# Cross queries and perceptron on unnormalised activations, with the token factor applied later

## The reference

```python
def rms_norm(x, g):
    return x * rsqrt(mean(x * x, axis=-1) + EPS) * g          # EPS = 1e-6

def memory_cross_attention(h, mem_n, wq, wkv, q_g, k_g, wo):
    q = rms_norm((h @ wq).reshape(b, s, XA_HEADS, XA_HEAD_DIM), q_g)
    kv = mem_n @ wkv
    ...

x = x + concatenate([y_a, y_b, y_c]) @ w_out                  # "mix_out"
x = x + memory_cross_attention(rms_norm(x, norm_cross), mem_n, ...)
hm = rms_norm(x, norm_mlp) @ mlp_w1
x = x + square(relu(hm)) @ mlp_w2
```

## Time and profile before

| | |
|---|---|
| median of 3 runs | 1986.47 us (1983.07 to 1989.07) |
| the profiled execution's own time | 1987.62 us |
| its span in the profile | 1985.7 us |
| TensorE busy | 1887.4 us, 95% |
| VectorE busy | 823.4 us, 41% |
| ScalarE busy | 457.4 us, 23% |
| GpSimd busy | 1110.6 us, 56% |
| mean granted TensorE clock | 0.966 of full |

### The profile page before, as it was taken

One profiled execution on the slowest core, in us unless ns is written; L12 is line 12 of the kernel. 1 busy time (PEld: TensorE's weight loads), 2 busy tenths in 40 slices (PEclk: granted clock), 3 DMA queues, 4 the chain that ended last, 5 costly groups with the idle time before them and its releaser, 6 DMA issues.

```text
span 1985.7 us, 27063 instructions
## 1 busy us (share of the span) xinstructions
PE 1887.4 (95%) x9670; PEld 1558.8 (79%) x9670; DVE 823.4 (41%) x1414; ACT 457.4 (23%) x933; POOL 1110.6 (56%) x856
## 2 busy tenths in 40 slices
PE   8999999998999999999998989989889869999998
PEld 4888888887888888888786768877768558887886
DVE  5642615364233333233414865964342653103300
ACT  3121111101222221222201155444122322001200
POOL 3745546496545544445464568752246468767862
PEclk9999999998999999999998989979898979999999
DMA  9423222383223222223222312010122123332331
GB/s 354 129 68 95 69 74 79 91 309 93 78 70 94 83 74 70 67 83 84 79 74 79 95 43 64 22 43 1 43 64 65 42 76 104 96 95 85 102 99 43
DMA packets 279468, 172.76 MB, mean 87 GB/s; under 512 B 5936, under 2 KB 269936, under 8 KB 278384
## 3 DMA queue, kind: packets, MB, share of 16 engines
q1 hardware_dynamic: 272912, 151.01, 26.0%
q10 hardware_dynamic: 6496, 20.93, 3.2%
HBM read 169.69 MB, written 2.10 MB: 87 GB/s over the span
## 4 chain that ended last, share of the span: by engine, by line
PE 88%; DVE 7%; ACT 2%; issue 1%; DMA 1%; POOL 1%; SPq 0%; DVEq 0%; ACTq 0%; POOLq 0%
PE acc L373 16%; PE acc L375 16%; PE acc L374 16%; PE acc L414 3%; PE acc L415 3%; PE acc L416 3%; PE acc L396 3%; PE st L427 3%; PE acc L398 3%; PE acc L397 3%; PE sc L1417 2%; PE ob L1347 2%; PE sc L1397 2%; PE bc L460 2%; DVE conv_out L2263 2%
## 5 line engine op out<-in xcount | busy, mean ns | idle before, releaser
L711 POOL TENSOR_TENSOR wl<-raw,wh 128x512 fp32r<-128x512 f32 x464 | 654.4, 1432 | 19.3
L708 POOL TENSOR_SCALAR wh<-raw 128x1024 fp32r<-128x1024 f32 x232 | 262.9, 1133 | 705.2 <-PE acc L375 312.3
L373 PE MATMUL acc<-hh,wh 128*128 128x512 f32 x816 | 331.7, 407 | 0.0
L375 PE MATMUL acc<-hh,wl 128*128 128x512 f32 x816 | 321.1, 393 | 0.0
L374 PE MATMUL acc<-hl,wh 128*128 128x512 f32 x816 | 320.2, 392 | 0.0
L373 PE MATMUL acc<-Yh,wh 128*128 128x512 f32 x512 | 204.3, 399 | 0.0
L374 PE MATMUL acc<-Yl,wh 128*128 128x512 f32 x512 | 203.2, 397 | 0.0
L375 PE MATMUL acc<-Yh,wl 128*128 128x512 f32 x512 | 203.2, 397 | 0.0
L373 PEld LDWEIGHTS acc<-hh,wh 128*128 128x128 f32 x816 | 155.0, 190 | 33.6 <-issue 1.9
L374 PEld LDWEIGHTS acc<-hl,wh 128*128 128x128 f32 x816 | 155.0, 190 | 33.0 <-issue 2.2
L375 PEld LDWEIGHTS acc<-hh,wl 128*128 128x128 f32 x816 | 154.5, 189 | 33.3
(11 more groups left out here) (411 smaller groups left out, 3061.3 us busy)
## 6 DMA issues: line engine op xcount, KB each, us to landing
raw<-in_att_w_in SPq DMA_DIRECT2D x64, 512.0 KB, 4.0
raw<-in_mlp_w SPq DMA_DIRECT2D x64, 512.0 KB, 3.8
raw<-in_ret_w_in SPq DMA_DIRECT2D x48, 512.0 KB, 3.9
ada_w<-in_ada_w ACTq DMA_DIRECT2D x8, 1536.0 KB, 8.1
raw<-in_w_in SPq DMA_DIRECT2D x23, 512.0 KB, 3.8
ada_w<-in_ada_w SPq DMA_DIRECT2D x16, 512.0 KB, 10.5
raw<-in_ret_w_out SPq DMA_DIRECT2D x16, 512.0 KB, 4.4
raw<-in_att_w_out SPq DMA_DIRECT2D x16, 512.0 KB, 4.1
```

Source lines behind the costliest of these rows:

```text
L373: e.matmul(bank[:, :], wh[:, s, k, :], rhs_high(k), start=(start and k == 0), stop=False)
L375: last = e.matmul(bank[:, :], wl[:, s, k, :], rhs_high(k), start=False, stop=(stop and k == k1 - 1))
L708: e.tensor_scalar(wh[:, s, :, :], raw[:, s, :, :], 1.0, 1.0, ALU.mult, ALU.mult).then_inc(high_done, 1)
L711: low = e.tensor_tensor(wl[:, s, k0:k0 + KT // 2, :], raw[:, s, k0:k0 + KT // 2, :], wh[:, s, k0:k0 + KT // 2, :].bitcast(F32), ALU.subtract)
```

## The change

For "nx": DVE adds a tile of mix_out to xT, ACT at once writes hh = xT times the gain (scale in the copy), DVE forms hl = xT times gain minus hh. No token factor goes in. TensorE's loop over the eight products is written out, and the memory's transposes stand between the products. The pair of queries then waits for the last add and for its tiles. The squares are summed beside that, and their columns go to st behind the pair ("nxcols"). The query roots take EPS (mean(x²) + EPS) in place of EPS, two small operations more. For "nf" the same: hh and hl come straight from xT, squares go to eight tiles of their own (fsq) and are summed by DVE behind the last hl; columns come behind mlp_in0, the root is squared, spread behind the second product of mlp_out0 and copied to fscale, and each output tile of both halves is multiplied by fscale in PSUM before it is added to xT.

```diff
+        def flat_high(e, tag, name, j, g):
+            e.wait_ge(*V.at(f"{name}x{j}"))
+            e.activation(hh[:, j, :], xT[:, j, :], ACT.Copy, scale=sm(g, j, 1)).then_inc(*AC.done(f"{tag}hi{j}"))
+        def flat_add(e, name, j):
+            e.wait_ge(unit_used, U[name] + j + 1)
+            e.tensor_tensor(xT[:, j, :], acc[j % 2][:, :], xT[:, j, :], ALU.add).then_inc(*V.done(f"{name}x{j}"))
+        def flat_low(e, tag, j, g):
+            e.wait_ge(*AC.at(f"{tag}hi{j}"))
+            e.scalar_tensor_tensor(out=hl[:, j, :], in0=xT[:, j, :], scalar=sm(g, j, 1), in1=hh[:, j, :].bitcast(F32),
+                                   op0=ALU.mult, op1=ALU.subtract).then_inc(*V.done(f"{tag}h{j}"))
...
 # ScalarE
-            out_squares(e, "mix_out", 2, 4)
-            for k in range(KT):
+            def memory_out(k):
                 e.wait_ge(*PE.at(f"m{k}"))
                 e.activation(mT[:, k, :], ob[k % 2][:, 0:MEM], ACT.Copy).then_inc(*AC.done(f"m{k}"))
-            norm_highs(e, "nx")
+            for j in range(KT):
+                flat_high(e, "nx", "mix_out", j, "norm_cross")
+                if j >= 2:
+                    e.wait_ge(*V.at(f"mix_outss{j - 2}"))
+                e.activation(sq[:, j % 2, :], xT[:, j, :], ACT.Square).then_inc(*AC.done(f"mix_outsq{j}"))
+                if j:
+                    memory_out(j - 1)
+            memory_out(KT - 1)
+            e.wait_ge(*V.at(f"mix_outss{KT - 1}"))
...
-            out_squares(e, "xa_out", 2, 4)
-            norm_highs(e, "nf")
+            for j in range(KT):
+                flat_high(e, "nf", "xa_out", j, "norm_mlp")
+            for j in range(KT):
+                e.activation(fsq[:, j, :], xT[:, j, :], ACT.Square).then_inc(*AC.done(f"nfsq{j}"))
             for half in range(2):
                 if half:
+                    e.wait_ge(*PE.at("nfbc"))
+                    e.activation(fscale[:, :], bc[:, :], ACT.Copy).then_inc(*AC.done("nfscale"))
...
 # TensorE
+            def out_flat(name, ready, k1, between=None):
                 e.wait_ge(*ready)
+                for j in range(KT):
+                    if j >= 2:
+                        e.wait_ge(*V.at(f"{name}x{j - 2}"))
+                    product(e, acc[j % 2], U[name] + j, U[name] + j, lambda k: Mh[:, k, :], lambda k: Ml[:, k, :], k1=k1)
+                    if between is not None and j:
+                        between(j - 1)
...
-            stream_sums(e, "nx", V.after("mix_outss3", 2))
...
-            norm_spread(e, "nx")
+            out_flat("mix_out", V.at(f"g_lo{GH - 1}"), KT, memory_turned)
+            memory_turned(KT - 1)
+            e.wait_ge(*V.at("mix_outx6"))
+            e.wait_ge(*V.at("mix_outx7"))
...
                 if h == 0:
+                    e.wait_ge(*V.at(f"mix_outss{KT - 1}"))
+                    columns(e, dg, 24, True, True, "nxcols")
                     square_sums(e, "nk", 2)
...
-            stream_sums(e, "nf", V.after("xa_outss3", 2))
-            norm_spread(e, "nf")
+            e.wait_ge(*V.at("xa_outx7"))
...
+                if half == 0:
+                    e.wait_ge(*V.at("nfss"))
+                    columns(e, dg, 0, "first", "last", "nfcols")
                 out_tensor(e, f"mlp_out{half}", [AC.after(f"f{half}r{b + 2}", 4) for b in range(2)],
-                           [V.after(f"f{half}yl3", 2), V.after(f"f{half}yl3", 4)])
+                           [V.after(f"f{half}yl3", 2), V.after(f"f{half}yl3", 4)],
+                           None if half else [lambda: None, lambda: norm_spread(e, "nf")])
...
 # VectorE
-            add_flat("mix_out")
-            norm_roots(e, "nx")
-            norm_vector(e, "nx", lambda k: sm("norm_cross", k, 1))
+            for j in range(KT):
+                flat_add(e, "mix_out", j)
+                flat_low(e, "nx", j, "norm_cross")
+                mix_out_sum(j)
...
-            rsqrt(e, 24, 1.0 / XD, "x_root")
+            e.tensor_scalar(rs[:, 2, 0:NT], st[:, 24:24 + NT], EPS / D, EPS * EPS, ALU.mult, ALU.add).then_inc(*V.done("nxeps"))
+            e.tensor_scalar(rs[:, 1, 16:24], st[:, 16:24], 1.0 / XD, EPS, ALU.mult, ALU.add).then_inc(*V.done())
...
+            roots(e, 0, 24, "x_root")
...
-            add_flat("xa_out")
-            norm_roots(e, "nf")
-            norm_vector(e, "nf", lambda k: sm("norm_mlp", k, 1))
+            for j in range(KT):
+                flat_add(e, "xa_out", j)
+                if j:
+                    flat_low(e, "nf", j - 1, "norm_mlp")
+            flat_low(e, "nf", KT - 1, "norm_mlp")
+            e.wait_ge(*AC.at("nfsq1"))
+            step(e, e.tensor_tensor(dg[:, :], fsq[:, 0, :], fsq[:, 1, :], ALU.add), V)
+            for j in range(2, KT):
+                e.wait_ge(*AC.at(f"nfsq{j}"))
+                step(e, e.tensor_tensor(dg[:, :], dg[:, :], fsq[:, j, :], ALU.add), V, "nfss" if j == KT - 1 else None)
+            def mlp_out(half):
+                c = U[f"mlp_out{half}"]
+                with e.Fori(0, KT // 2) as i:
+                    V.enter(f"mlp_out{half}", i)
+                    for b in range(2):
+                        x = xT[:, bass.ds(i * 2 + b, 1), :]
+                        e.wait_ge(unit_used, c + i * 4 + b + 3)
+                        step(e, e.tensor_tensor(acc[b][:, :], acc[b][:, :], fscale[:, :], ALU.mult), V)
+                        e.tensor_tensor(x, acc[b][:, :].unsqueeze(1), x, ALU.add).then_inc(*V.done(f"mlp_out{half}x{b}"))
+                    V.leave(KT // 2)
```

More of the change, by code:

```diff
@@ L309, in build @@
         xP = at("xa_probs_t", [P, 2, 2, S], 96 * KB)
+        fsq = at("mlp_squares", [P, KT, S], W)
+        fscale = at("mlp_scale", [P, S], W + 16 * KB)
         kidx_in, levels_in, dsa_w_in = sem("kidx_in"), sem("levels_in"), sem("dsa_w_in")
@@ L1854, in _, with memory_turned @@
                 spread(e, f"g_obc{t}", c0=4 * t, bank=(bc, sc[0])[t % 2])
-            def out_flat(name, ready, k1):
+            def out_flat(name, ready, k1, between=None):
                 e.wait_ge(*ready)
[L1858 to L1866, removed]
-            stream_sums(e, "nx", V.after("mix_outss3", 2))
-            e.wait_ge(mem_in, 16)
-            for k in range(KT):
-                e.wait_ge(*(AC.at(f"m{k - 2}") if k >= 2 else V.at(f"g_lo{GH - 1}")))
+                for j in range(KT):
[4 more added lines that the diff above has]
+                        between(j - 1)
+            def memory_turned(k):
+                if k == 0:
+                    e.wait_ge(mem_in, 16)
+                if k >= 2:
+                    e.wait_ge(*AC.at(f"m{k - 2}"))
                 for t in range(2):
@@ L2583, in _, with mix_out_sum @@
             low(3)
[L2585 to L2594, removed]
-            add_flat("mix_out")
-            norm_roots(e, "nx")
-            norm_vector(e, "nx", lambda k: sm("norm_cross", k, 1))
+            def mix_out_sum(j):
+                e.wait_ge(*AC.at(f"mix_outsq{j}"))
+                if j == 0:
+                    e.tensor_copy(dg[:, :], sq[:, 0, :]).then_inc(*V.done("mix_outss0"))
+                else:
+                    e.wait_ge(*V.at(f"mix_outss{j - 1}"))
+                    e.tensor_tensor(dg[:, :], dg[:, :], sq[:, j % 2, :], ALU.add).then_inc(*V.done(f"mix_outss{j}"))
+            for j in range(KT):
+                flat_add(e, "mix_out", j)
+                flat_low(e, "nx", j, "norm_cross")
+                mix_out_sum(j)
             norm_roots(e, "nk", MEM)
@@ L2603, in _ @@
             e.wait_ge(*PE.at("x_cols7"))
-            rsqrt(e, 24, 1.0 / XD, "x_root")
+            e.tensor_scalar(rs[:, 2, 0:NT], st[:, 24:24 + NT], EPS / D, EPS * EPS, ALU.mult, ALU.add).then_inc(*V.done("nxeps"))
+            e.tensor_scalar(rs[:, 1, 16:24], st[:, 16:24], 1.0 / XD, EPS, ALU.mult, ALU.add).then_inc(*V.done())
+            e.wait_ge(*V.at("nxeps"))
+            step(e, e.scalar_tensor_tensor(out=rs[:, 1, 0:16].rearrange("p (h t) -> p h t", h=XH),
+                                           in0=st[:, 0:16].rearrange("p (h t) -> p h t", h=XH), scalar=1.0 / XD,
+                                           in1=rs[:, 2, 0:NT].unsqueeze(1).to_broadcast([P, XH, NT]),
+                                           op0=ALU.mult, op1=ALU.add), V)
+            roots(e, 0, 24, "x_root")
             step(e, e.tensor_scalar(rs[:, 0, 0:16], rs[:, 0, 0:16], XD ** -0.5, None, ALU.mult), V)
@@ L2656, in _ @@
                     V.leave(4)
-                out_vector(e, f"mlp_out{half}", None, sums=False)
+                if half == 0:
+                    e.wait_ge(*PE.at("nfcols"))
+                    step(e, e.tensor_scalar(rs[:, 1, 0:NT], st[:, 0:NT], 1.0 / D, EPS, ALU.mult, ALU.add), V)
+                    roots(e, 0, NT, None)
+                    step(e, e.tensor_tensor(rs[:, 0, 0:NT], rs[:, 0, 0:NT], rs[:, 0, 0:NT], ALU.mult), V, "nfroot")
+                    e.wait_ge(*AC.at("nfscale"))
+                mlp_out(half)
     return {"PE": (PE.marks), "AC": AC.marks, "V": V.marks, "G": G.marks, "VG": VG.marks}
```

## The result

The changed kernel takes 1965.74 us (median of 4 runs, 1960.14 to 1967.28), against 1986.88 for the kernel before in the same comparison: a ratio of 0.9899, 95% interval 0.9878 to 0.9920. The forecast was 1966.7.

A forecast was written before the change was run, and what follows sets the result against it. TensorE, busy for 95% of the span, was taken as the bound, so edits pay where it idles, runs at half clock or changes instruction count. Gains of 9.5 (part A) and 10.3 (part B), 19.8 us, gave a median of 1966.7, range 1961.5 to 1973.5.

The forecast's parts named there:

- part B: xa_out to perceptron: the pair gains 13.9 us, less 1.05, 1.05 and 1.5 given back, 10.3 us in all.
- Transposes between products: In mix_out, six pairs of memory transposes between products cost 2.2 us (1.9 to 3.6); two pairs are free.
- DVE behind each product: In mix_out, DVE takes some 3.5 us per product of 5.6, so its work stays covered at no price.
- The start of the perceptron's pair: Behind xa_out, TensorE could start at 1597.0, do six matmuls, then stall from 1598.9 for the second unit's split.
- The split of the second unit: GpSimd's split of mlp_in0's second unit takes 5.0 us and ends at 1602.4 (1601.3 to 1603.1).
- The rule on the shared read interface: Two-input DVE and GpSimd SBUF reads contend, the second waiting; taken to its end, split ends 1603.1, time 0.7 us higher.
- The slow start: At the perceptron's pair, half clock behind the stall costs 2.0 us (0 to 3.5).
- Given back: Part B's costs: nfcols behind mlp_in0 1.05, nfbc in mlp_out0 1.05, TensorE waits behind each half's last tile 1.5 us.
- Full clock in B (1): Rival: the clock stays full through the stall at the perceptron's pair; 1964.7 us, chance 0.16.
- A longer hold-up of GpSimd (2): Rival: second split ends two microseconds later, half clock lasts two slow starts; 1970.7 us, chance 0.12.
- A long slow stretch (3): Rival: a 20.4 us half-clock stretch stays, costing 10.2 us: 1974.9, chance 0.06; at both places 1985, 0.04.
- one through all of mlp_in0 (4): Rival: TensorE held at half clock for mlp_in0's 384 matmuls, 77 us; time 2044, chance 0.04.

The follow-up runs named there:

- e8: Changed kernel with the sixteen memory transposes in one block behind the eighth product; 51.92 us from first mix_out matmul to query pair.
- e3: Changed kernel with each of the eight nf squares on ACT right behind its copy to hh; 1961.97 us (4 runs).
- e6: Changed kernel with the memory's squares in own tiles, summed by DVE during the query pair; 8.64 us from the memory's sums to third query unit.
- e9: Changed kernel with half splits for xa_out and nf's squares each behind its copy; 111.79 us from first xa_out to first mlp_out0 matmul.
- e10: Changed kernel with half xa_out splits, nf's squares between copies, memory's norm early, its column sums inside the query pair; 1944.65 us, ratio 0.9791.
- e5: Changed kernel with GpSimd splitting only the four used k-tiles of each xa_out unit; 117.57 us from first xa_out to first mlp_out0 matmul.
- e4: Changed kernel without six of the seven DVE sums over the squares of nf; 1960.59 us in one run.
- e2: Changed kernel with only the perceptron's norm changed, the queries' norm as in the kernel before; 1976.42 us, ratio 0.9951.

## Why the prediction was right, step by step

The time came out 1.0 us under the forecast, and most terms came out near theirs; one step of part B was wrong in its course, and that the sum held there was luck. The gain was 21.1 us by the medians and 21.3 by the stretches, where 19.8 was forecast; part of that is hidden in the time, since the median of the kernel before was 1986.88 in this comparison and 1986.47 in the forecast.

- **The wait for the last add**, 1.35: 1.23.
- **Transposes between products**, 2.2 (1.9 to 3.6): 1.2 for twelve, under the lower bound. Of the 3.29 for twelve in the earlier trace rows, which gave the upper one, some two thirds were then alternation with ACT, as in the block of e8.
- **The pair at full clock**, 11.1: 10.98. The clock didn't fall over the hole ahead.
- **nxcols**, 1.05: 0.81 from start to start.
- These four gave 10.9 us in the first two stretches, where 9.5 was forecast. The third row of the table gives 0.4 back: behind nxcols the granted clock was 0.63 over 1471.6 to 1477.6 and 0.50 over 1477.7 to 1486.4, and the memory's eight sums took 6.06 us where they had taken 4.47. I had called this hole unchanged; nearly so.
- **DVE behind each product** of mix_out was put at 3.5 us. It is 0.69 for the add, 0.79 of waiting for ACT, 1.65 for hl and 1.78 for the sum, 4.9 of 5.82, beside GpSimd's splits. The cover held with 0.97 us to spare, not with 2.
- **The start of the perceptron's pair** is the step that failed. I read "PE acc L396 <- ACT hh" in the earlier trace rows as a wait for the first tile, when the first tile of hl was ready at 1612.2 by DVE's timeline and the pair started at 1614.85. That row was already the count three steps ahead of the loop. Followed into the code, it would have shown what stands there in the changed kernel.
- **The split of the second unit**, expected 29.3 us behind xa_out's first matmul (1602.4 there): it ended 28.8 behind it, at 1585.2. Since the pair had started late and at half clock, it reached the second unit at 1586.4, and the stall that I had priced never showed. Late start and stall replace each other, so the pair's end came 18.14 us behind the last product's start, where 18.30 was forecast. The sum was right by luck: two waits of different cause happened to end within 1.5 us of each other (1583.7 and 1585.2). In e3, whose course is the forecast one, the pair's end came 17.40 behind.
- **The rule on the shared read interface** (the Trainium skill, "SBUF", "Who interferes with whom") agrees in kind: 4.88 and 4.82 us from split to split with the sums, 3.92 with one of them left. Taken to its end it gave 5.6 for a split; the rows gave 4.9, my 5.0 was nearer.
- **The slow start**, 2.0 (0 to 3.5): the pair took 13.6 us instead of 10.9, 2.7; in e6, behind the same wait, 12.4. (The idle time that had brought the clock down before was 3.00 us, by the bracket of 1599.06, not the 3.2 that I had read.)
- **Given back**: nfcols and nfbc 1.05 each, measured 0.80 each. The boundaries 1.5: TensorE's idle time ahead of mlp_in1 went from 1.20 to 1.93 us, ahead of the output from 0.91 to 1.64, 1.46 in all, and the multiply into PSUM takes 0.70. The bound for that multiply could have been narrower. What it lacked was a slow start behind the longer idle time, 1.6 us in four other profiles; that the clock would not fall again before the output holds for both profiles of the changed kernel, not for those four.
- **The rivals.** Full clock in B (1) fell in the changed kernel and came true only in e9 and e10, once both waits were gone. A longer hold-up of GpSimd (2) didn't come, its split ended 0.5 us early. A long slow stretch (3) or one through all of mlp_in0 (4) didn't come: 1.00 from 1589.5 to 1673.4.

```profile
1583.80:1588.90 5.10, 5.10 (x12) 4.08 (x13) 5.00 (x4) 1.43 (x3) 5.02 (x4) 0.50 0.38 107
1589.50:1673.40 83.90, 83.90 (x372) 69.45 (x371) 33.96 (x33) 18.07 (x30) 70.26 (x48) 1.00 0.33 97
```

That ACT's and GpSimd's waits were the only two is shown by e3, e5 and e9. What decides in an execution whether 1300 to 1325 runs at 0.59 or 0.89 stays open.

## What to carry to other kernels

When a chain of latencies is taken out, list everything that the next instruction waits for, also the waits that cost nothing in the old trace: a semaphore count written for a loop's earlier turn means, in its first turn, whatever stands in front of the loop. Of two waits that end within a microsecond of each other, taking away one shows nothing; try both together before calling either harmless. And compare profiles by stretches from a matmul in them, since the spans of two executions can differ by 6 us from clock alone; and look at the granted clock inside a stretch before 1 or 2 us of it are put down to an edit.

## What the runs showed of the hardware

- Of six DVE operations on two columns that ran while GpSimd split weights, four took 0.96 to 1.19 us; when it was idle, they took 0.16 to 0.17 (e6 and e10). A root of nine such steps took 1.73 us or 5.30, by where it was put.
- GpSimd's split slows too: 3.6 us from split to split with DVE idle (1469.78 to 1473.37 in the changed kernel), 3.9 beside one sum (e4), 4.8 to 4.9 beside back-to-back sums.
- TensorE stayed at full clock behind an idle time of 1.19 us (e9), and through 4.8 us of sparse transposes with one idle time of 1.89 in them (e8); it was found at half behind an idle time of 4.1 us (the changed kernel twice, e2, e4, e5, e6, e8). Behind 1.93 us it stayed full in six profiles and was at half within 1.5 us of the restart in four. In e3 idle times of 1.35 and 2.79 us with six matmuls between were followed by four matmuls near full pace and then seven at half (1587.07 to 1590.06).
